# Two mixed layers: attention and output projection in one program, values with v stationary, head norms per block

## What is computed

```python
r_o = rms_norm(retention(...)).reshape(b, s, RET_WIDTH)            # 4 heads of 64
sc = (einsum(qn, k_nope) + einsum(qp, k_pe)) * scale               # 8 heads, 64 + 32 wide
p = softmax(where(mask, sc, -inf)); m_o = einsum(p, v)             # v: 64 wide
g_o = rms_norm(gla(...), gla_norm[l]).reshape(b, s, GLA_WIDTH)     # 4 heads of 64
mixed = concatenate([r_o * silu(rz), m_o * silu(mz), g_o * silu(gz)])
x = x + gate * (mixed @ w_out[l])
```

## Time and profile before

| | us |
|---|---|
| median of 3 runs (lowest, highest) | 4241.92 (4230.81, 4244.13) |
| the profiled execution | 4239.87 |
| its span, first to last instruction | 4238.1 |
| PE, DVE, POOL, ACT busy | 3753.3, 1551.3, 1157.9, 1012.8 |
| first mixed layer: attention (`ma`), up to its last value matmul | 3077.0 to 3265.2 |
| from there to the first matmul of the output projection | 57.7 |
| the same stretch in the second mixed layer | 57.6 |

### The profile page before, as it was taken

One profiled execution on the slowest core, in us unless ns is written; L12 is line 12 of the kernel. 1 busy time (PEld: TensorE's weight loads), 2 busy tenths in 40 slices (PEclk: granted clock), 3 DMA queues, 4 the chain that ended last, 5 costly groups with the idle time before them and its releaser, 6 DMA issues. The chain is left out here.

```text
span 4238.1 us, 45022 instructions
## 1 busy us (share of the span) xinstructions
PE 3753.3 (89%) x17816; PEld 2919.9 (69%) x17816; DVE 1551.3 (37%) x2013; ACT 1012.8 (24%) x1552; POOL 1157.9 (27%) x670
## 2 busy tenths in 40 slices
PE   6995777799999999999999996899798769988967
PEld 6873555688888888788888884776466558754735
DVE  2123666431111139642111124544244431523453
ACT  2002665210100124521001011132244111313520
POOL 3221441233233226533332331223000322210031
PEclk9997788899999999999999997899899879998978
DMA  3122330111111121211111111131322022113111
GB/s 103 50 79 86 116 113 26 45 50 45 50 49 45 49 89 50 80 45 49 50 45 49 49 45 70 40 99 41 94 61 82 27 95 65 55 44 93 58 61 59
DMA packets 77716, 264.95 MB, mean 63 GB/s; under 512 B 9328, under 2 KB 10512, under 8 KB 77584
## 3 DMA queue, kind: packets, MB, share of 16 engines
q1 hardware_dynamic: 52160, 182.91, 14.3%
q10 hardware_dynamic: 18512, 55.08, 3.7%
q0 software_dynamic: 6912, 25.17, 1.9%
HBM read 211.48 MB, written 47.45 MB: 61 GB/s over the span
## 5 line engine op out<-in xcount | busy, mean ns | idle before, releaser
L1119 POOL CAST tk_w_hi<-tk_w_raw 128x1024 fp32r<-128x1024 f32 x160 | 178.9, 1118 | 1185.4 <-PE tk_acc L191 551.3
L191 PE MATMUL tk_acc<-tk_b_hi,tk_w_hi 128*128 128x512 f32 x1280 | 397.6, 392 | 10.4 <-POOL tk_w_lo L1121 10.4
L191 PE MATMUL tk_acc<-tk_a_hi,tk_w_hi 128*128 128x512 f32 x1280 | 399.4, 393 | 3.9 <-POOL tk_w_lo L1121 3.1
L191 PE MATMUL tk_acc<-tk_b_lo,tk_w_hi 128*128 128x512 f32 x1280 | 399.7, 394 | 0.0
L191 PE MATMUL tk_acc<-tk_a_lo,tk_w_hi 128*128 128x512 f32 x1280 | 399.2, 393 | 0.0
L1121 POOL TENSOR_TENSOR tk_w_lo<-tk_w_raw,tk_w_hi 128x1024 fp32r<-128x1024 f32 x160 | 394.2, 2464 | 12.8
L191 PE MATMUL tk_acc<-tk_a_hi,tk_w_lo 128*128 128x512 f32 x1280 | 396.6, 391 | 0.0
L191 PE MATMUL tk_acc<-tk_b_hi,tk_w_lo 128*128 128x512 f32 x1280 | 395.9, 390 | 0.0
L1266 ACT ACTIVATE tk_sq<-tk_r 128x1024 f32<-128x1024 f32 x64 | 68.0, 1062 | 1078.6 <-DVE tk_r L1384 1078.6
L1359 DVE TENSOR_TENSOR xT<-tk_acc,xT 128x1024 f32<-128x1024 f32 x80 | 98.0, 1225 | 617.7 <-PE tk_acc L191 617.7
L191 PEld LDWEIGHTS tk_acc<-tk_b_hi,tk_w_hi 128*128 128x128 f32 x1280 | 240.8, 188 | 61.6 <-POOL tk_w_lo L1121 10.8
(11 more groups left out here) (374 smaller groups left out, 6719.7 us busy)
## 6 DMA issues: line engine op xcount, KB each, us to landing
tk_w_raw<-in_w_trunk SPq DMA_DIRECT2D x160, 512.0 KB, 3.6
da_w_mod<-in_ada_w POOLq DMA_DIRECT2D x48, 512.0 KB, 3.9
pj_w_raw<-in_w_in SPq DMA_DIRECT2D x44, 512.0 KB, 3.6
qk_w_raw<-in_w_qkv SPq DMA_DIRECT2D x24, 512.0 KB, 3.7
x_dram<-xT ACTq DMA_DIRECT2D x24, 512.0 KB, 5.8
qk_dram<-qk_o ACTq DMA_DIRECT2D x16, 512.0 KB
proj_dram<-acc ACTq DMA_DIRECT2D x32, 256.0 KB, 2.0
xT<-x_dram SPq DMA_DIRECT2D x16, 512.0 KB, 11.7
```

The costliest lines, as they stand in the source:

```text
L191: last = pe.matmul(self.acc[:, u, s * HALF:(s + 1) * HALF], w[:, u, k, :], h[:, k, s * HALF:(s + 1) * HALF], start=(k == order[0] and part ...
L1119: pool.tensor_copy(pn.hi[:, u, :, :], pn.raw[:, u, :, :]).then_inc(sems[f"w_hi{u}"], 1)
```

## The change

In `mixed_front`, `column_sums` multiplies by the full block of ones `bd`, so each head's sum stands on all its 64 rows; after every block ACT takes the root (`head_root`) and DVE the reciprocal and the scaling of the block in place (`head_norm`). Only the four gates of the attention are stored; those of retention and GLA stay in the core, and DVE multiplies with them (`gated`, and two at the end). The projection's weights are reordered so that the attention's gates come first.

`mixed_back` joins `ma` and `mw`. DVE scales the exponentials before the transposes (`normalise`). Values of a step are one group for both heads, v stationary (64 columns), `pts` moving, each head on its own half of the output rows, which is already feature-major: the output transposes go. POOL multiplies a unit by its gate, ACT and DVE split it (`high`, `low`) while the next unit runs; the last unit goes from the longest block to the shortest, in two halves. Retention and GLA are split at the start. The products use the score buffer and start with chunks 0, 1, 6, 7.

```diff
-        order = [c.k for c in self.prep.chunks] if self.prep else list(range(self.kc))
+        order = order or ([c.k for c in self.prep.chunks] if self.prep else list(range(self.kc)))
...
                     def column_sums(b, r):
                         pe.wait_ge(sems[f"{r}_oc"], b + 1)
+                        if b or r == "l":
+                            pe.wait_ge(sems["l_root" if r == "l" and b else "r_root"], b if b else SB)
                         for tt in range(2):
-                            last = pe.matmul(p_st[:, tt, b, :], sqo[:, b % 2, tt, :], self.bd[:, 0:P:64],
-                                             start=(b == 0 and tt == 0), stop=True, skip_group_check=True)
+                            last = pe.matmul(p_st[:, tt, :], self.bd[:, :], sqo[:, b % 2, tt, :], start=True, stop=True)
                         last.then_inc(sems[f"{r}_cs"], 1)
...
-                            pe.wait_ge(sems["r_sums"], 1)
...
-                        if n:
+                        if 1 <= n <= 4:
                             act.wait_ge(sems[f"g_out{s}"], 16 * n)
-                        act.activation(go[:, s, :], acc[:, 0, s * HALF:(s + 1) * HALF], ACT.Silu)\
-                            .then_inc(sems["g_taken"], 1)
-                        act.wait_ge(sems["g_taken"], i + 1)
-                        act.dma_start(self.proj[P_GATES + n, :, s * HALF:(s + 1) * HALF], go[:, s, :])\
-                            .then_inc(sems[f"g_out{s}"], 16)
+                        if n == 5:
+                            act.wait_ge(sems["r_gated"], s + 1)
+                        dst = go[:, s, :] if n < 6 else ab[:, 0, n - 6, s * HALF:(s + 1) * HALF]
+                        act.activation(dst, acc[:, 0, s * HALF:(s + 1) * HALF], ACT.Silu).then_inc(sems["g_taken"], 1)
+                        if n < 4:
+                            act.wait_ge(sems["g_taken"], i + 1)
+                            act.dma_start(self.proj[P_GATES + n, :, s * HALF:(s + 1) * HALF], dst)\
+                                .then_inc(sems[f"g_out{s}"], 16)
+                    def head_root(b, r):
+                        act.wait_ge(sems[f"{r}_cs"], b + 1)
+                        if b or r == "l":
+                            act.wait_ge(sems["l_rn" if r == "l" and b else "r_rn"], b if b else SB)
+                        act.activation(rt[:, :, :], p_st, ACT.Sqrt, bias=self.const("eps6"), scale=1.0 / 64)\
+                            .then_inc(sems[f"{r}_root"], 1)
...
                             gate(SB + b - 1)
+                            head_root(b - 1, "l")
...
+                    def head_norm(b, r, oT, gain):
+                        dve.wait_ge(sems[f"{r}_root"], b + 1)
+                        link(dve.reciprocal(rt[:, :, :], rt[:, :, :]))
+                        x = oT[:, :, b * P:(b + 1) * P]
+                        if gain is None:
+                            ins = dve.tensor_tensor(x, x, rt[:, :, :], ALU.mult)
+                        else:
+                            ins = dve.scalar_tensor_tensor(x, x, gain, rt[:, :, :], ALU.mult, ALU.mult)
+                        ins.then_inc(sems[f"{r}_rn"], 1)
+                    def gated(i):
+                        j, s = divmod(i - SB, 2)
+                        dve.wait_ge(sems["g_taken"], i + 1)
+                        x = o_ret[:, j, s * HALF:(s + 1) * HALF]
+                        dve.tensor_tensor(x, x, go[:, s, :], ALU.mult).then_inc(sems["r_gated"], 1)
...
+                        if b:
+                            head_norm(b - 1, "r", o_ret, None)
...
+                        if b == 0:
+                            head_norm(SB - 1, "r", o_ret, None)
+                            dve.wait_ge(sems["r_rn"], SB)
+                        else:
+                            head_norm(b - 1, "l", o_gla, self.col("gla_norm", layer))
+                        if 1 <= b <= 4:
+                            gated(SB + b - 1)
+                    head_norm(SB - 1, "l", o_gla, self.col("gla_norm", layer))
+                    dve.wait_ge(sems["l_rn"], SB)
+                    dve.wait_ge(sems["g_taken"], 2 * SB)
+                    for j in range(2):
+                        dve.tensor_tensor(o_gla[:, j, :], o_gla[:, j, :], ab[:, 0, j, :], ALU.mult)
...
+    def mixed_back(self, tag, layer, v, o_ret, o_gla):
...
+        down = sorted(ORDER, reverse=True)
+        blocks = [(u, b) for u in range(units) for b in (ORDER if u < units - 1 else down)]
+        nb = len(blocks)
...
+            hi = sb("hi", [P, DK, S], F32R)
+            lo = sb("lo", [P, DK, S], F32R)
...
+            halves = [(u, 0, S) for u in range(units - 1)] + [(units - 1, HALF, S), (units - 1, 0, HALF)]
+            done_at = [SB, 2 * SB, 3 * SB, 3 * SB + 4, 4 * SB]
+            order = [0, 1, 6, 7, 2, 3, 4, 5]
...
+                        if u >= 2:
+                            sync.wait_ge(sems["gated"], u - 1)
+                        sync.dma_start(zg[:, u % 2, :], self.proj[P_GATES + u]).then_inc(sems[f"z_in{u % 2}"], 16)
+                        load(u)
+                    sync.wait_ge(sems["scores"], 2 * nb)
+                    for n in range(DK):
+                        sync.dma_start(self.xT[:, n, :], self.x_dram[n]).then_inc(sems[f"x_ld{n}"], 16)
+                    for p in range(units, DK):
+                        load(p)
...
+                    for n in range(4):
+                        src, kk = (o_ret, n) if n < 2 else (o_gla, n + 4)
+                        pool.wait_ge(sems["s_hi"], n + 1)
+                        pool.tensor_tensor(lo[:, kk, :], src[:, n % 2, :], hi[:, kk, :].bitcast(F32), ALU.subtract)\
+                            .then_inc(sems["s_lo"], 1)
+                    weights(0)
+                    weights(1)
+                    for i, (u, a, b) in enumerate(halves):
+                        pool.wait_ge(sems["out"], done_at[i])
+                        pool.wait_ge(sems[f"z_in{u % 2}"], 16 * (u // 2) + 16)
+                        pool.tensor_tensor(o[:, u % 2, a:b], o[:, u % 2, a:b], zg[:, u % 2, a:b], ALU.mult)\
+                            .then_inc(sems["gated"], 1)
+                    for p in range(2, DK):
+                        weights(p)
...
+                        pe.wait_ge(sems["prob"], i + 1)
+                        if i:
+                            pe.wait_ge(sems["pts"], i)
...
+                    def values(t):
...
+                        u, b = blocks[t]
+                        pe.wait_ge(sems["pts"], 2 * t + 2)
+                        if t >= 2:
+                            pe.wait_ge(sems["out"], t - 1)
+                        for j in range(b + 1):
+                            for m in range(2):
+                                at = u * P + 64 * m
+                                last = pe.matmul(ov[64 * m:64 * m + 64, t % 2, 0:P], v[:, j, at:at + 64],
+                                                 pts[:, m, j * P:(j + 1) * P], start=(j == 0), stop=(j == b))
+                        last.then_inc(sems["pv"], 1)
+                    for t in range(-1, nb + 1):
+                        scores(t + 1, 0)
+                        values(t - 1)
+                        transposes(t, 0)
+                        scores(t + 1, 1)
+                        transposes(t, 1)
+                    def ready(kk):
+                        if kk in (0, 1, 6, 7):
+                            pe.wait_ge(sems["s_lo"], order.index(kk) + 1)
+                        else:
+                            pe.wait_ge(sems["o_lo"], kk - 1 if kk < 5 else 5)
+                    pn.credit(pe)
+                    pe.wait_ge(sems["exp"], 2 * nb)
+                    for p in range(DK):
+                        pn.product(pe, p % 2, p // 2, hi, lo, ready if p == 0 else None, order)
...
+                    def normalise(t, m):
...
+                        dve.wait_ge(sems["exp"], 2 * t + m + 1)
+                        r = st[:, t % 4, 3, m:m + 1]
+                        link(dve.reciprocal(r, st[:, t % 4, 2, m:m + 1]))
+                        dve.tensor_scalar(span(t, m), span(t, m), r, None, ALU.mult).then_inc(sems["prob"], 1)
+                    def output(t):
...
+                        u, b = blocks[t]
+                        if u >= 2 and t % SB == 0:
+                            dve.wait_ge(sems["o_lo"], u - 1)
+                        dve.wait_ge(sems["pv"], t + 1)
+                        dve.tensor_copy(o[:, u % 2, b * P:(b + 1) * P], ov[:, t % 2, 0:P]).then_inc(sems["out"], 1)
...
+                    for t in range(-1, nb + 2):
+                        maximum(t + 1, 0)
+                        normalise(t, 1)
+                        maximum(t + 1, 1)
+                        normalise(t + 1, 0)
+                        output(t - 1)
+                        if t % SB == 5 and t > SB:
+                            low(t // SB - 1)
+                    low(3)
+                    low(4)
...
+                    def copies(t, m):
...
```

(30 more changed lines are left out.)

178 lines of the change are left out of this document (155 added, 23 removed).

## The result

The changed kernel takes **4099.57 us** (median of 4 runs, 4098.92 to 4101.7) against 4239.9 for the one before in the same comparison (4 runs, 4230.81 to 4244.13): ratio 0.9665, 95% interval 0.9629 to 0.970. The forecast was 4111 with a range of 4080 to 4148. The profiled execution took 4100.22 us, 139.7 less than the profiled one of before; the sum had said 128.6.

The account below looks back on a forecast made before the run. PE, busy for 89% of the span, was taken as the bound; -57.4 - 0.7 - 23.9 + 10.2 + 7.5 = -64.3 us a layer, -128.6 for two, from 4239.87 to 4111 us; range 4080 to 4148.

Parts of the forecast that it names:

- The stretch: Between attention and products: the 57.7 us with PE mostly waiting go or move under the attention, -57.4 us a layer.
- Low clock of the first products: First two matmuls of the products: with no gap before them they run at full clock, -0.7 us a layer.
- The values: Joined attention: values with v stationary in 64 columns, and no output transposes, save PE time, -23.9 us a layer.
- the change of form: Values of each attention step: 0.16 us going into the narrow form and 0.11 coming out, 8.6 us a layer.
- Full overlap: Rival, attention values: both heads' tiles run wholly side by side, 0.107 us a key block of both heads; 4080 us, chance 0.06.
- Waits: Joined attention: PE waits for the softmax chain, short rows, casts, low parts and the last unit's end, +10.2 us a layer.
- The rival in which the softmax chain binds and the clock falls: Joined attention: waits drop the clock, a unit takes 47.5 us; 4165 us, halfway 4138; chance 0.16.
- The front: Retention and GLA blocks and their end: wider column sums, table loads, root, reciprocal and scaling add +7.5 us a layer.
- The tail: End of the front stage: last table load, root, reciprocal, scaling, two products and a barrier add +4.2 us a layer.
- The second front: Start of layer 2's front stage: counted among the rest of the network, which has no edit; no term.
- The lower end of the case: Whole kernel: 4085 us, the forecast with no waits and cheap changes of form.

Follow-up runs that it names:

- late_first: Changed kernel with the products of the joined stage taking the last head pair's chunk first instead of last; 4103.8 us, one run.
- sqrt_ready: Changed kernel with ACT taking a one-column root after the joined attention's last cast, so the root table loads under the products; 4099.6 us, two runs.
- same_half: Changed kernel with values computed one head after the other, both heads writing output rows 0 to 63, output copied in two pieces; 4151.2 us (ratio 0.978).
- junk_between: Changed kernel with values computed head by head and one small full-form matmul between the heads in steps of 2 to 8 blocks; 4166.3 us, one run.
- lo_on_dve: Changed kernel with the four low parts of retention and GLA made by DVE in attention steps 6 to 9, instead of POOL in the first; 4087.9 us (0.9629).

## Why the prediction was right, and where not

- **The stretch, -57.4.** Right: 57.7 us became 0.17, and late_first shows that the chain of the last half unit costs 3.58 us where nothing hides it.
- **Low clock of the first products, -0.7.** Wrong in layer 1, where the products took 0.9 us more than before; 1.0 less in layer 2. Why the clock falls behind nearly the same short waits (0.35 to 0.56 us) in one layer and not in the other, and in sqrt_ready in the other and not in the one, stays open.
- **The values, -23.9.** That neighbours on two halves overlap is shown by same_half, and 0.214 a key block was 0.218. But 0.214 was twice the 0.107 of one matmul, which I had scaled down from 512 columns; same_half shows that a matmul of 128 columns by itself costs 0.218, and only the overlap brings two of them to what their columns cost in the long stream. That the two figures meet is luck; the better source was the 0.37 of GLA, which is what a step of one key block costs here. Mis-sized was the change of form: 0.27 a step, put together from two differences in other stages, measured 0.15. A unit's values are 36 x 0.218 + 8 x 0.153 = 9.1 us in place of 9.9, 3.3 less a layer, so the term is -27.2. The warning of the Trainium skill (TensorEngine Tiling (Array Packing), Key Properties), that a change of mode drains the engine, holds in junk_between: the overlap is lost at it. At 0.15 us its price for 32 steps is 4.9 us a layer, not 8.6.
- **Full overlap, 4080.** It fell: a key block of both heads costs 0.218, not 0.107. The same page of the Trainium skill, that tiles work in parallel, agrees with same_half, where a pair costs twice as much; but a single matmul costs 0.218 and not the 0.107 that this rival took for it, so the halving ends at 0.218 a pair.
- **Waits, +10.2.** The sum was near by luck: with -27.2 for the values, what was left over is 6.7 us in layer 1 and 13.3 in layer 2. What the chain and the short rows really cost is about 3 us a layer: lo_on_dve's attention is 24.3 us shorter than the 188.2 of the earlier trace rows, of 27.2 that the values give, and a unit has PE idle for 1.0 us where I had 1.8. The rest was not in the prediction at all: POOL's subtractions, 3.2 and 8.0 us, and in layer 2 a longer low clock at the start of the stage. The step that failed is "the splits of retention and GLA, made in the first steps", which I costed at 0.5 a unit on ACT and DVE, without asking what POOL's instruction does to DVE beside it. The rival in which the softmax chain binds and the clock falls had low clock inside a unit right, and the cause wrong: lo_on_dve keeps the chain and loses the low clock, and units two to four never had it.
- **The front, +7.5.** The tail was 4.8 (4.2 predicted), the two table loads are there in every block, and PE waits no longer for ACT than before (1.1 us a layer in place of 1.3). In the blocks I had +3.3 and the sum is 0.1 and 0. The rows of after show two things that cancel. A block is 0.05 us longer for the wider column sums where I took 0.13, and three retention blocks run 0.25, 0.5 and 1.0 us late; PE waits 0.74 and 0.29 us there for DVE's `pj_at`; I put that down to the head norm in DVE's queue, and no run tested it. On the other side the turn from retention to GLA got 2.3 us shorter: before, PE waited there 0.76 and 0.56 us for ACT and then ran some 5 us at the low clock; the second wait is gone and so is the low clock.
- **The second front, 0.** It costs 2.9 us at its start, 1.6 of them given back behind it: ACT held the table of exponentials, so the root needs a load of 1.28 us, and the diagonal, 1.3 us later, met POOL's subtraction. The change had taken the stage that ended with the root's table away, and I did not ask which table was left behind.

In all: -7.2 for the two attentions, -6.5 for the front's blocks, +1.2 for the tails, +1.3 each for the products' clock and the second front, and spread in stages that nobody touched (the projection before layer 2's attention is 1.6 shorter) make the 11 us between 128.6 and 139.7. So the total is nearer than its terms: values 6.6 us too small over the two layers and blocks 6.5 too high, against things that were not in the sum at all. The lower end of the case was also mis-added: without waits (20.4) and with cheap changes of form (17.6) the terms give 4073, not 4085.

## What to carry to other kernels

Narrow matmuls pay when their neighbours write different halves of the output, and should come in long runs, since a visit to the narrow form costs a fixed time. When work moves to POOL under a chain of DVE, ask what POOL runs at the moment of the chain's shortest step; here a subtraction of 1024 columns turned a 0.3 us step into 1.8, and the low clock behind the wait of 1.6 us cost between as much as the wait and four times that. When a stage is removed, look at what it left behind for the next one, such as ACT's function table, and at which queue issues DMAs ahead of a computation that others wait for. And before a total that came out right is trusted, hold each of its terms against the profile.
